# Two layers of a hybrid decoder trunk on one core: the order in which one DMA queue issues weights and modulation tiles

## The chip, the core and the metric

The kernel runs on one core of a Trainium2 chip. A core has TensorE (matrix products, PE in the profile), VectorE (DVE), ScalarE (ACT), GpSimd (POOL), SyncE (SP, which here issues nearly all transfers from HBM) and 16 DMA engines. The metric is the device time of one launch in microseconds (us); lower is better.

## The reference

Two layers work on x, 256 tokens of width 2048, in f32. With c one vector of 2048, each layer computes

```
mod = silu(c) @ ada_w + ada_b            # ada_w: 2048 x 12288, six vectors of 2048: shift, scale, gate, twice
h = rms_norm(x, norm_mix) * (1 + sc_a) + sh_a
p = h @ w_in                             # inputs of three attention mixers
o = concat(rms(mla(p)), rms(fox(p)), rms(nsa(p)))
x = x + gt_a * (o @ w_out)
h = rms_norm(x, norm_mlp) * (1 + sc_m) + sh_m
x = x + gt_m * (square(relu(h @ mlp_w1)) @ mlp_w2)    # mlp width 8192
```

and a last RMSNorm follows. The product `silu(c) @ ada_w` has a single row, but its weights are 100 MB per layer; the other weights are some 215 MB per layer. Every weight is read from HBM once.

## The kernel before, in words

**Pieces.** All products of the tokens with weights are cut into 828 pieces, numbered Q = 0 to 827 in `PIECES`: 158 in the front part of each layer (`ORDER`: input projection, latent projections, compression, output projection) and 256 in each MLP. A piece is two blocks of 128 rows of a weight by at most 512 columns (512 KB where it is full). It passes four stations: SP loads it into `w_raw` (a ring of `RAW` = 5 slots, line 613); ACT rounds it into `w_hi` (line 724); DVE subtracts, `w_lo = w_raw - w_hi` (line 1188); PE multiplies with both (lines 1659 to 1661, or 1679 and 1680 for the compression weights). `w_hi` and `w_lo` are rings of `RING` = 4 slots: ACT starts on piece Q when PE is done with Q - 4. A slot of `w_raw` is free when the DVE instruction of piece Q - 5 is done (`lo_done`).

**Modulation tiles.** The product with `ada_w` is done on DVE: 384 tiles of 128 x 1024 (512 KB), n = 0 to 383, sixteen to a block. Each is multiplied by one column of silu(c) and added to `ada_acc` (line 1125 for the first tile of a block, 1128 for the others); PE then sums `ada_acc` over the partitions (line 1569). The first 64 tiles go through a ring of `FIRST_RING` = 8 slots in `arena` (line 628). All later ones go through `ada_raw`, which has 2 slots (line 633): tile n can be loaded when tile n - 2 is used (`ada_used`). All loads of tiles and pieces are issued by SP, in one queue.

**The order on DVE.** `SIDE` lists for each piece the further steps after it; DVE does `w_lo` of piece Q, then the steps of `SIDE[Q]`. `DVE_ORDER` is that list, reduced to the entries ("lo", Q) and ("ada", n). Tiles 0 to 15 come ahead of piece 0, tiles 16 to 63 lie three to a piece among pieces 1 to 17, and the later blocks are spread over 14 to 70 pieces each: 16 over 16 or 17 pieces at the end of the first layer's front part and at the start of its MLP, eight blocks of 16 over 21 pieces each (with 3 pieces between) in the rest of that MLP. After piece 572 (the second layer's MLP) there are tiles for the first 54 pieces only.

**The order on SP.** `LOADS` (lines 366 to 377) has one entry per load: the place in `DVE_ORDER` of the step that frees its slot, the place of the step that reads it, the kind, the number. SP goes through `LOADS` in order; `load_piece` and `load_ada` wait for the slot's semaphore and issue the transfer. A wait holds up everything behind it on SP. The list is sorted by its first member, the freeing step, so that SP waits for events in the order in which DVE makes them.

Of the kernel before, what the change touches and what calls it, by code (L numbers as in the profile page):

```python
# [366 lines left out]
LOADS = []  # L367
# [3 lines left out]
for n in range(TILES):  # L371
# [2 lines left out]
    else:  # L374
        free = DVE_AT["ada", n - 2] if n >= FIRST_TILES + 2 else DVE_AT["ada", n - FIRST_RING]
    LOADS.append((free, DVE_AT["ada", n], "ada", n))
LOADS.sort()


Y_SLOT, Y_NO, Y_BEFORE = {}, {}, {}  # L380
# [1413 lines left out]
```

How the kernel before makes its waits and increments, by code:

```python
        def free_y(eng, l, name):  # L582
            before = Y_BEFORE[l, name]
            if before is not None and before[0] == l and before[1] in Y_LAST_T:
                eng.wait_ge(*t_is_full(l, Y_LAST_T[before[1]]))
                if before[1] in Y_LAST_SPLIT:
                    eng.wait_ge(split_done, split_value(l, Y_LAST_SPLIT[before[1]]))
# [6 lines left out]
            def load_piece(Q):  # L595
# [6 lines left out]
                        src = mlp_w2[l, s * D + 256 * p:s * D + 256 * p + 256, 512 * (ch - 4):512 * (ch - 4) + 512]  # L602
                    n = 512
                elif chunk == "cw1":
                    w1, n = (cmp_k_w1, cmp_v_w1)[p // 16], 512
                    src = w1[l, 256 * (p % 16):256 * (p % 16) + 256, :]
                else:
                    w, c0, n, a_ = CHUNKS[chunk]
                    row = P * OUT_KT[p] if w == "w_out" else 256 * p
                    src = w_rows[w][l, row:row + 256, c0:c0 + n]
                if Q >= RAW:
                    sp.wait_ge(lo_done, Q - RAW + 1)
                sp.dma_start(w_raw[:, Q % RAW, :, 0:n], src.rearrange("(k p) n -> p k n", p=P)
                             ).then_inc(raw_landed[Q % RAW], 16)
# [1 line left out]
            def load_ada(n):  # L616
# [8 lines left out]
                if n < FIRST_TILES:  # L625
                    if n >= FIRST_RING:
                        sp.wait_ge(ada_used, n - FIRST_RING + 1)
                    sp.dma_start(first_raw[:, n % FIRST_RING, :].rearrange("p (s d) -> p s d", s=2), src
```

## Time and profile before

| what | value |
|---|---|
| time, median of 3 runs (lowest to highest) | 2499.36 us (2497.02 to 2499.56) |
| the profiled execution's own time | 2493.08 us |
| its span, first to last instruction | 2490.8 us |
| TensorE clock granted, mean over the span | 0.984 of full |
| busy: PE, DVE, ACT | 96%, 71%, 48% of the span |
| read from HBM | 629.85 MB |

How to read it: the profile is one execution; "idle before" is the time an engine stood still ahead of an instruction, with what ended it. Busy PE is modelled from pipelined matmuls. "To landing" is the time from a transfer's issue on SP to its semaphore. Transfers of the first 120 us are bound by the DMA engines; behind that the DMA engines have room.

### The profile page before, as it was taken

The numbers are of one execution on the slowest core, as the hardware profiler recorded it, in microseconds if no ns is written. First come the engines' busy times: TensorE is split into PE (matmuls) and PEld (weight loads), VectorE is DVE, ScalarE is ACT, GpSimd is POOL, SyncE is SP. The second block draws the span as 40 slices with busy tenths as digits, with TensorE's granted clock in tenths as the row PEclk, the third lists the DMA queues.
The fourth block names the chain that finished last, engine by engine and source line by source line (L and its number), as shares of the span: only waits on it lengthen the run. The fifth ranks groups of instructions, "written<-read, shape, count | busy, mean of one in ns | idle before, by whom it ended". The sixth has DMA issues, their size and how long they took to land.

```text
span 2490.8 us, 29668 instructions
## 1 busy us (share of the span) xinstructions
PE 2388.0 (96%) x11277; PEld 1977.1 (79%) x11277; DVE 1773.2 (71%) x2116; ACT 1202.6 (48%) x1646; POOL 23.7 (1%) x50
## 2 busy tenths in 40 slices
PE   3799999989999999999999999999999999999998
PEld 3678888767778878888888888877788888888887
DVE  7988988678777777787777788676566545555555
ACT  3256555435534434434445566454563453443453
POOL 1000000000000000000000000000000000000000
PEclk9799999999999999999999999999999999999999
DMA  9979986688889989889877788466577656656664
GB/s 367 380 244 349 311 272 216 224 278 278 296 305 314 309 289 324 295 298 317 297 248 254 260 286 272 144 208 212 187 243 245 193 179 198 190 185 195 183 190 144
DMA packets 318612, 633.91 MB, mean 254 GB/s; under 512 B 20428, under 2 KB 41352, under 8 KB 317832
## 3 DMA queue, kind: packets, MB, share of 16 engines
q1 hardware_dynamic: 314432, 625.49, 75.7%
q10 hardware_dynamic: 4040, 6.54, 0.8%
q8 instruction: 90, 1.47, 0.2%
q14 instruction: 50, 0.41, 0.0%
HBM read 629.85 MB, written 2.10 MB: 254 GB/s over the span
## 4 chain that ended last, share of the span: by engine, by line
PE 78%; DVE 10%; DMA 7%; issue 3%; ACT 2%; SPq 0%; POOL 0%; ACTq 0%; POOLq 0%; DVEq 0%
PE acc L1659 17%; PE acc L1661 17%; PE acc L1660 17%; PE pair L1659 6%; PE pair L1661 6%; PE pair L1660 6%; DMA ada_raw<-in_ada_w 4%; DVE ada_acc L1128 4%; DVE w_lo L1188 3%; DMA arena<-in_ada_w 2%; PE bank_T L1524 1%; PE bank_T L1569 1%; PE pair L1707 1%; PE acc L1679 1%; PE acc L1680 1%
## 5 line engine op out<-in xcount | busy, mean ns | idle before, releaser
L1188 DVE TENSOR_TENSOR w_lo<-w_raw,w_hi 128x1024 fp32r<-128x1024 f32 (+3 forms) x828 | 978.5, 1191 | 321.4 <-ACT w_hi L724 320.6
L724 ACT ACTIVATE w_hi<-w_raw 128x1024 fp32r<-128x1024 f32 (+3 forms) x828 | 849.1, 1032 | 719.4 <-PE acc L1661 460.1
L1659 PE MATMUL acc<-w_hi,hT_hi 128*128 128x512 f32 (+3 forms) x1536 | 611.2, 398 | 28.6 <-DVE hT_lo L1302 15.2
L1661 PE MATMUL acc<-w_lo,hT_hi 128*128 128x512 f32 (+3 forms) x1536 | 591.8, 385 | 0.0
L1660 PE MATMUL acc<-w_hi,hT_lo 128*128 128x512 f32 (+3 forms) x1536 | 590.5, 384 | 0.0
L1128 DVE SCALAR_TENSOR_TENSOR ada_acc<-ada_raw,silu_c,ada_acc 128x1024 f32<-128x1024 f32 x300 | 383.9, 1280 | 99.2 <-DMA ada_raw<-in_ada_w 97.7
L1659 PEld LDWEIGHTS acc<-w_hi,hT_hi 128*128 128x128 f32 x1536 | 293.1, 191 | 90.9 <-DVE hT_lo L1302 18.0
L1661 PEld LDWEIGHTS acc<-w_lo,hT_hi 128*128 128x128 f32 x1536 | 292.2, 190 | 56.5
L1660 PEld LDWEIGHTS acc<-w_hi,hT_lo 128*128 128x128 f32 x1536 | 293.5, 191 | 52.2 <-issue 1.7
L1659 PE MATMUL acc<-w_hi,uT_hi 128*128 128x512 f32 (+1 forms) x720 | 283.3, 394 | 0.9 <-DVE w_lo L1188 0.9
L1661 PE MATMUL acc<-w_lo,uT_hi 128*128 128x512 f32 (+1 forms) x720 | 279.6, 388 | 0.0
L1660 PE MATMUL acc<-w_hi,uT_lo 128*128 128x512 f32 (+1 forms) x720 | 279.5, 388 | 0.0
L1659 PE MATMUL pair<-w_hi,hT_hi 128*128 128x512 f32 (+1 forms) x448 | 178.9, 399 | 15.9 <-DVE w_lo L1188 15.9
L1661 PE MATMUL pair<-w_lo,hT_hi 128*128 128x512 f32 (+1 forms) x448 | 174.1, 389 | 0.0
L1660 PE MATMUL pair<-w_hi,hT_lo 128*128 128x512 f32 (+1 forms) x448 | 173.8, 388 | 0.0
L1659 PEld LDWEIGHTS acc<-w_hi,uT_hi 128*128 128x128 f32 x720 | 135.2, 188 | 30.0 <-DVE w_lo L1188 2.2
L1661 PEld LDWEIGHTS acc<-w_lo,uT_hi 128*128 128x128 f32 x720 | 135.1, 188 | 27.9
L1660 PEld LDWEIGHTS acc<-w_hi,uT_lo 128*128 128x128 f32 x720 | 135.2, 188 | 27.7 <-issue 1.0
L1659 PE MATMUL pair<-w_hi,uT_hi 128*128 128x512 f32 (+1 forms) x352 | 137.0, 389 | 2.4 <-DVE w_lo L1188 2.3
L1661 PE MATMUL pair<-w_lo,uT_hi 128*128 128x512 f32 (+1 forms) x352 | 136.2, 387 | 0.0
L1660 PE MATMUL pair<-w_hi,uT_lo 128*128 128x512 f32 (+1 forms) x352 | 136.1, 387 | 0.0
L1659 PEld LDWEIGHTS pair<-w_hi,hT_hi 128*128 128x128 f32 x448 | 86.0, 192 | 35.0 <-DVE w_lo L1188 19.4
(259 smaller groups left out, 2038.0 us busy)
## 6 DMA issues: line engine op xcount, KB each, us to landing
w_raw<-in_mlp_w SPq DMA_DIRECT2D x512, 512.0 KB, 4.8
ada_raw<-in_ada_w SPq DMA_DIRECT2D x320, 512.0 KB, 5.1
w_raw<-in_w_in SPq DMA_DIRECT2D x112, 512.0 KB, 4.9
arena<-in_ada_w SPq DMA_DIRECT2D x64, 512.0 KB, 11.3
w_raw<-in_w_out SPq DMA_DIRECT2D x64, 512.0 KB, 5.0
w_raw<-in_nsa_cmp_k_w SPq DMA_DIRECT2D x32, 512.0 KB, 5.1
w_raw<-in_nsa_cmp_v_w SPq DMA_DIRECT2D x32, 512.0 KB, 5.1
w_raw<-in_w_in SPq DMA_DIRECT2D x16, 388.0 KB, 4.8
```

What stands on the lines that cost most here:

```text
L724: a.activation(w_hi[:, Q % RING, :, 0:n], w_raw[:, Q % RAW, :, 0:n], ACT.Copy).then_inc(hi_done, 1)
L1128: ins = v.scalar_tensor_tensor(ada_acc[:], raw, silu_c[:, kt:kt + 1], ada_acc[:], ALU.mult, ALU.add)
L1188: v.tensor_tensor(w_lo[:, Q % RING, :, 0:n], w_raw[:, Q % RAW, :, 0:n], w_hi[:, Q % RING, :, 0:n].bitcast(F32), ALU.subtract).then_inc(lo_ ...
L1524: mm = pe.transpose(bank[:, k, P * m:P * m + P], halves[m], ident[:])
L1569: mm = pe.matmul(flat_[:, k:k + 1], ada_acc[:, P * k:P * k + P], ones[:, 0:1], start=True, stop=True)
L1659: pe.matmul(o, st_hi[:, kt + k, tok], wh, start=first and k == 0, stop=False)
L1660: pe.matmul(o, st_lo[:, kt + k, tok], wh, start=False, stop=False)
L1661: mm = pe.matmul(o, st_hi[:, kt + k, tok], wl, start=False, stop=last and k == 1)
L1679: pe.matmul(acc[1][:, j, :], st, w_hi[:, Q % RING, k, :], start=kt == 0, stop=False)
L1680: mm = pe.matmul(acc[1][:, j, :], st, w_lo[:, Q % RING, k, :], start=False, stop=kt == 31)
L1707: mm = pe.matmul(o, NQ[:, h, qt], k_[:, h // 4, 0:keys], start=True, stop=True)
```

## The change

`LOADS` is sorted by its second member, the place in `DVE_ORDER` of the step that reads the load, in place of the step that frees its slot. Slots, waits and semaphores are the same; 861 of the 1212 loads stand at another place of the list.

```
@@ -374,7 +374,7 @@
     else:
         free = DVE_AT["ada", n - 2] if n >= FIRST_TILES + 2 else DVE_AT["ada", n - FIRST_RING]
     LOADS.append((free, DVE_AT["ada", n], "ada", n))
-LOADS.sort()
+LOADS.sort(key=lambda load: load[1])
```

Two stretches of the list, worked out from the code (w is a piece, a a tile):

```
before: a57 a58 a59 w19 a60 a61 a62 w20 a63 a64 a65 w21
after:  a57 w16 a58 a59 a60 w17 a61 a62 a63 w18 w19 w20

before: w148 a141 w149 a142 w150 a143 w151 a144 w152 a145 w153 a146 a147 w154
after:  w148 a144 a145 w149 a146 w150 a147 w151 a148 w152 a149 w153 a150
```

## Rows read from the trace of the kernel before

**Rows 1.** The page: busy time by engine, and PE's share in 40 slices.

```profile
PE 2388.0 (96%) x11277; PEld 1977.1 (79%) x11277; DVE 1773.2 (71%) x2116; ACT 1202.6 (48%) x1646; POOL 23.7 (1%) x50
PE   3799999989999999999999999999999999999998
```

**Rows 2.** Stretches: from:to, length, busy by engine (instructions), clock, DMA share, GB/s.

```profile
30.00:120.00 90.00, 64.69 (x280) 56.00 (x281) 80.40 (x79) 31.90 (x46) 0.35 (x1) 0.83 1.05 384
500.00:580.00 80.00, 68.78 (x299) 54.24 (x298) 58.19 (x63) 35.78 (x59) 1.10 (x2) 0.96 0.76 249
...
660.00:1280.00 620.00, 617.43 (x2824) 509.89 (x2824) 473.91 (x431) 276.29 (x293) 0.00 (x0) 1.00 0.89 302
1900.00:2400.00 500.00, 500.00 (x2247) 413.13 (x2246) 262.71 (x226) 226.94 (x236) 0.00 (x0) 1.00 0.62 188
```

**Rows 3.** Waits of engines, whole span: us in total, times, longest us.

```profile
ACT w_hi L724 <- PE acc L1661: 460.1, 312, 4.9
...
DVE ada_acc L1128 <- DMA ada_raw<-in_ada_w: 97.7, 73, 3.2
```

**Rows 4.** Waits of the SP queue, whole span.

```profile
SPq L613 <- DVE w_lo L1188: 1322.6, 810, 8.4
SPq L633 <- DVE ada_acc L1128: 537.0, 298, 7.3
```

**Rows 5.** Waits between 30 and 130 us.

```profile
DVE ada_acc L1128 <- DMA arena<-in_ada_w: 5.1, 9, 1.2
```

**Rows 6.** DVE in order of time, 121 to 126 us: start, us, instruction, idle before.

```profile
121.71 1.29 DVE L1128 SCALAR_TENSOR_TENSOR ada_acc<-arena,silu_c,ada_acc 128x1024 f32<-128x1024 f32 x1 [0.23 <-DMA arena<-in_ada_w]
122.91 2.36 DVE L1188 TENSOR_TENSOR w_lo<-w_raw,w_hi 128x1024 fp32r<-128x1024 f32 x2
125.18 0.16 DVE L1142 TENSOR_TENSOR ada_A<-bank_T,bcols 128x8 f32<-128x8 f32 x1
```

**Rows 7.** SP, ACT in order of time, 668 to 673 us.

```profile
668.48 0.34 SPq L633 DMA_DIRECT2D ada_raw<-in_ada_w  x1
669.62 0.37 SPq L613 DMA_DIRECT2D w_raw<-in_mlp_w  x1
670.81 0.34 SPq L633 DMA_DIRECT2D ada_raw<-in_ada_w  x1
...
672.18 1.05 ACT L724 ACTIVATE w_hi<-w_raw 128x1024 fp32r<-128x1024 f32 x1
```

**Rows 8.** Time to landing: tiles in the whole span, pieces 570:620, pieces 620:660.

```profile
DMA to landing us min/median/max: 3.4/5.1/11.1
DMA to landing us min/median/max: 3.8/5.2/6.2
DMA to landing us min/median/max: 4.8/5.3/7.2
```

**Rows 9.** DVE in order of time, around seven late pieces (first, two, last).

```profile
222.59 0.74 DVE L1125 TENSOR_SCALAR ada_acc<-ada_raw,silu_c 128x1024 f32<-128x1024 f32 x1
...
526.08 0.75 DVE L1125 TENSOR_SCALAR ada_acc<-ada_raw,silu_c 128x1024 f32<-128x1024 f32 x1 [3.50 <-PE bank_T L1569]
...
530.64 1.28 DVE L1128 SCALAR_TENSOR_TENSOR ada_acc<-ada_raw,silu_c,ada_acc 128x1024 f32<-128x1024 f32 x1 [1.28 <-DMA ada_raw<-in_ada_w]
531.84 1.22 DVE L1188 TENSOR_TENSOR w_lo<-w_raw,w_hi 128x1024 fp32r<-128x1024 f32 x1
...
619.82 1.28 DVE L1128 SCALAR_TENSOR_TENSOR ada_acc<-ada_raw,silu_c,ada_acc 128x1024 f32<-128x1024 f32 x1 [1.07 <-DMA ada_raw<-in_ada_w]
...
901.82 1.28 DVE L1128 SCALAR_TENSOR_TENSOR ada_acc<-ada_raw,silu_c,ada_acc 128x1024 f32<-128x1024 f32 x1
```

**Rows 10.** PE in order of time: first matmuls of pieces 60, 150, 179, 276.

```profile
230.24 0.50 PE L1679 MATMUL acc<-w_hi,uT_hi 128*128 128x512 f32 x1 [0.32 <-DVE w_lo L1188]
...
533.20 0.47 PE L1659 MATMUL acc<-w_hi,hT_hi 128*128 128x512 f32 x1 [0.76 <-DVE w_lo L1188]
...
628.51 0.50 PE L1659 MATMUL acc<-w_hi,hT_hi 128*128 128x512 f32 x1
...
911.26 0.50 PE L1659 MATMUL pair<-w_hi,uT_hi 128*128 128x512 f32 x1 [0.82 <-DVE w_lo L1188]
```

More of the change, by code:

```diff
@@ L376 @@
     LOADS.append((free, DVE_AT["ada", n], "ada", n))
-LOADS.sort()
+LOADS.sort(key=lambda load: load[1])
 Y_SLOT, Y_NO, Y_BEFORE = {}, {}, {}
```

## The prediction, written before the changed kernel ran

> **What bounds the kernel now.** I read the page first, then the time by stretches, the waits (of the engines, then of SP), the landing times, and last single instructions at the places where PE has little in hand.
>
> The page has PE busy for 2388.0 of 2490.8 us; the slices show that the missing 103 us lie mostly in the first two, with an 8 for 498 to 560 us and one at the end [rows 1]. By stretches: from 30 to 120 us PE works 64.7 of 90 us while the DMA engines are full (share 1.05, 384 GB/s) and DVE is busy for 80.4; from 500 to 580 us, the seam between front part and MLP of the first layer, PE works 68.8 of 80; in the rest of that MLP 617.4 of 620, though DMA still runs at 0.89; in the second layer's MLP all of 500, with DMA at 0.62 [rows 2]. So PE is the bound, except at the start (transfers and DVE) and at the seams (DVE in turn with PE).
>
> Two waits say how the pieces are covered. ACT waits 460.1 us for PE before it makes w_hi: the weight is there and the 4-slot ring behind it is full, which is the reserve. DVE waits 97.7 us for modulation tiles, 73 times, nearly all while PE doesn't stop [rows 3]: the two-slot ring of the tiles has little reserve, and the pieces' ring pays for it. SP is idle most of the time, waiting for lo_done (1322.6 us) and ada_used (537.0 us) [rows 4]; each transfer leaves the moment its slot is free. That is what the change gives up.
>
> **The change, part by part.** No instruction is added or removed; 1212 loads, the same slots and semaphores. Three effects.
>
> 1. *The start.* Up to tile 63 the DMA engines are full, so a load lands when the bytes ahead of it have passed. Tile 63 stood behind pieces 0 to 20, now behind 0 to 17: pieces 18, 19 (524 KB each) and 20 (328 KB) are 1.376 MB less, at 384 GB/s [rows 2] 3.6 us. Tile 63 was waited for at 121.71 [rows 6] and now lands at 118.1. But DVE next makes w_lo of pieces 18 and 19, which now stand behind it: 118.1 + 2 x 1.37 (524 KB at 384 GB/s) = 120.8, then w_hi 1.05 [rows 7] and w_lo 1.22, plus 0.1 of semaphores: 123.2, where it was 122.91 + 2.36 = 125.27 [rows 6]. Gain 2.1 us. DVE waited 5.1 us for tiles in this phase [rows 5], so its own work isn't what stops the gain. Bounds: nothing (if another step sets piece 18) to 3.6 us (all of it). I take 2.1, the one that the rows of this spot give step by step. Tiles 31 and 47 gain likewise, but it is the same 1.376 MB, and not added.
>
> 2. *Pieces lose lead.* A tile n of the two-slot ring can't be issued before tile n - 2 is used. In the new list every piece that DVE reads after tile n stands behind it, with its slot free or not. From the order of the list: 355 of 828 pieces are issued later than before, 18 in the first 24, 88 in the rest of the first front part, 204 in the first MLP, 45 in the second front part, none in the second MLP. Their lead falls from 5 pieces to 3 or 4. Behind such a piece wait its w_hi on ACT (and ACT's later steps: evacuations, exponentials), its w_lo on DVE (and the tiles and additions behind that), and then PE. The few loads that ACT issues aren't behind SP.
>
> A held piece is ready for PE at: use of the freeing tile + 0.4 (SP issues the tile first, 0.34 [rows 7]) + landing L + w_hi 1.05 + w_lo 1.22 [rows 9] + 0.1 = +2.8 + L. PE loses what that is past its first matmul on the piece. Worked for piece 150: it stands behind tile 146, which waits for tile 144, used at 526.08 + 0.75 = 526.83; PE starts at 533.20 [rows 9, 10]: 6.4 us, so it is late when L is over 3.6. I did this for all held pieces and took the worst of each cluster (a later one is shifted with it). With L = 6.0 (need 8.8):
>
> piece 60: 223.33 to 230.24, 6.9, late 1.9
> piece 150: 6.4, late 2.4
> piece 155: 543.98 to 551.29, 7.3, late 1.5
> piece 165: 578.94 to 586.46, 7.5, late 1.3
> piece 179: 621.10 to 628.51, 7.4, late 1.4
> piece 211: 716.84 to 724.07, 7.2, late 1.6
> piece 276: 903.10 to 911.26, 8.2, late 0.6
>
> [rows 9, 10] have the first, the second, the fifth and the last of the seven. Sum 10.7 us; the others are covered by PE's reserve.
>
> Why 6.0: pieces land in 5.2 and 5.3 us (medians) in these stretches, the quickest in 3.8, the slowest in 7.2 [rows 8]. Before, a piece left 1.14 us behind a tile (668.48, 669.62 [rows 7]), now 0.37, so 0.8 us more of the tile's bytes are ahead of it: 5.2 + 0.8. Bounds of the sum: with the quickest of 3.8 it is 0.2; with 7.2 each of the seven has 1.2 more and some ten more pieces come over, 26 us.
>
> 3. *Tiles land sooner.* The piece that used to leave 1.2 us ahead of a tile (669.62 before 670.81 [rows 7]) now leaves with the tile before, so a tile finds up to 0.8 us less in front of it. DVE waits for tiles just where PE's reserve is gone (1.28 at 530.64, 1.07 at 619.82 [rows 9]). Bounds: nothing, to 5 us (0.8 at each of the six late places from 150 on). I take 2: most of it is used up by the wait for the piece, which is later.
>
> The skill bears on 2. The rows of SP show waits of 1322.6 and 537.0 us on its own sequencer [rows 4]. The Trainium skill, DMA: Bandwidth & Descriptors, "Anatomy of one DMA — SWDGE (gpsimd) path", says that DMA engines never wait on semaphores: the wait is on the issuing sequencer, ahead of dispatch; by that rule a held tile stops every piece behind it though its slot is free, and the trace agrees. The same section fits a transfer as about 2.0 us + bytes/436e3; for 524 KB that is 3.2 us, an estimate from that page, and with it as L no piece would be late and the sum would be -2.1 - 2 = -4. The quickest tile of the trace took 3.4 and the median 5.1 [rows 8], so in this traffic the measured L decides.
>
> Sum: -2.1 + 10.7 - 2 = +6.6 us. The profiled execution took 2493.08 and would be 2499.7; it lies 6.3 under the median of the runs, 2499.36, on which I put the forecast: 2506.
>
> **The rivals.**
>
> *A. The cover holds (not slower).* One mechanism, at pieces 150 to 211: the tile comes first and lands in time, DVE runs ahead, and the pieces' later issue falls into PE's reserve. For it: PE stops hardly at all in the first MLP [rows 2] and ACT has 460 us of waiting for PE [rows 3]; L under 5.2 is enough to halve the sum (5.3, from the same list). Against it: the reserve is at 0.1 us just at these places (PE ends its idle time on w_lo at 230.24, 533.20, 911.26 [rows 10]). With L about 4.9: start -3.6, pieces +3.5, tiles -5: -5 us, 2494. It decides from L = 5.2 downward.
>
> *B. DVE falls behind for good (much slower).* Three tiles now make a loop: use of tile n - 2, issue 0.4, landing of the piece behind tile n, w_hi 1.05, 0.1, w_lo 1.22, tile n + 1 1.28: 4.1 + L. PE needs 2.67 us a piece (500 us for 2247/12 pieces [rows 2]), 3.5 us a tile at 16 tiles to 21 pieces. With L = 6.0 the loop gives 3.4 us a tile, just enough; with 7.2 it gives 3.75, and loses 4 us in each of nine blocks, of which the reserve takes most, and PE some 1 to 2; with the 26 us above less 2.1 and 2 it is +22 to +30: 2525. Against: the median piece isn't near 7.2.
>
> *C. It does nothing that shows*, since nearly all of the 355 pieces have more than 8.8 us: 2499.4.
>
> **How the numbers follow.** No change can be told within 0.2%, 5 us of the median (2494.4 to 2504.4). My forecast, 0.55, has its own range +1 to +14 (2500 to 2513); some 0.37 of that is over +5, 0.18 within. A 0.27: 0.12 faster by over 5 us, 0.15 within. B 0.14, slower. C 0.04, within. Together: faster 0.12, same 0.37, slower 0.51. The range for 8 in 10 runs from -6 (A) to +20 (the near end of B): 2493 to 2519.
>
> **What would show it.** Right: in the trace after, SP's waits on ada_used grow at the cost of those on lo_done; DVE's wait for tiles falls well under 97.7 us, and ACT's waits for w_raw transfers, and DVE's for w_hi, grow; the ada_A instruction of 125.18 comes at 123; PE first idles on w_lo near pieces 60, 150 to 186 and 211; the second layer's MLP is unchanged to 1 us. Wrong: PE without new idle time from 220 to 920 us (A), or with more in every block up to 1280 (B); landings of pieces that stay at 5.2 or under though they leave with a tile; a start that isn't earlier at tile 63, which would mean that slots, not bytes, pace it.

## The result: 14 us slower, and the profile after

| | before | after |
|---|---|---|
| median (5 runs each) | 2498.19 us | 2509.48 us |
| lowest to highest | 2495.92 to 2499.56 | 2507.36 to 2512.72 |
| ratio, 95% interval | | 1.0056 (1.0044 to 1.0067): 11 to 17 us |
| profiled execution, its span | 2493.08, 2490.8 | 2507.36, 2505.1 |

The median lies in the range (2493 to 2519) and the sign is as forecast; the size is about twice the 6.6 us of the sum, which forecast 2506. (The ratio, taken round by round on one chip, makes 14 us; the two medians alone differ by 11.3.)

The page of the changed kernel, PE's line, PE's slices and the two groups of section 5 whose idle time moved (columns: busy us, mean ns, then idle us before and what ended most of it):

```profile
PE 2388.8 (95%) x11277; PEld 1972.7 (79%) x11277; DVE 1783.9 (71%) x2116; ACT 1201.6 (48%) x1646; POOL 23.8 (1%) x50
PE   3799999989999999999999999999999999999998
...
L724 ACT ACTIVATE w_hi<-w_raw 128x1024 fp32r<-128x1024 f32 (+3 forms) x828 | 851.0, 1033 | 886.4 <-DMA w_raw<-in_mlp_w 336.7
...
L1128 DVE SCALAR_TENSOR_TENSOR ada_acc<-ada_raw,silu_c,ada_acc 128x1024 f32<-128x1024 f32 x300 | 383.6, 1279 | 17.3 <-DMA ada_raw<-in_ada_w 15.6
```

PE works as long as before [rows 1]; only its idle time grew. DVE's waits for tiles fell from 97.7 us [rows 3] to 15.6. In their place ACT waits for pieces (13.8 us for those of the MLPs before, 336.7 now). The engines' waits over the whole span (us in total, times, longest), and those of the SP queue:

```profile
DVE w_lo L1188 <- ACT w_hi L724: 428.8, 438, 4.2
ACT w_hi L724 <- DMA w_raw<-in_mlp_w: 336.7, 181, 8.4
ACT w_hi L724 <- PE acc L1661: 273.7, 197, 3.6
```

```profile
SPq L613 <- DVE w_lo L1188: 996.0, 518, 8.8
SPq L633 <- DVE ada_acc L1128: 732.5, 248, 14.3
```

ACT's wait for PE, the sign of a full reserve, fell from 460.1 us [rows 3] to 273.7; SP's waits moved from lo_done to ada_used [rows 4].

The stretches that answer to [rows 2], shifted with the program (500 to 584 answers to 500 to 580, 669 to 1294 to 660 to 1280, 1914 to 2414 to 1900 to 2400; their ends fit to 1 to 3 us, so the exact loss is read from the table below):

```profile
30.00:120.00 90.00, 65.19 (x290) 56.66 (x291) 82.99 (x82) 30.20 (x45) 0.60 (x1) 0.85 1.05 384
500.00:584.00 84.00, 69.10 (x286) 53.45 (x285) 56.02 (x60) 34.89 (x57) 1.10 (x2) 0.92 0.68 231
...
669.00:1294.00 625.00, 618.02 (x2818) 507.70 (x2817) 478.76 (x429) 270.51 (x289) 0.00 (x0) 1.00 0.86 299
1914.00:2414.00 500.00, 500.00 (x2247) 413.16 (x2246) 262.89 (x227) 226.88 (x235) 0.00 (x0) 1.00 0.62 189
```

This stretch of the second MLP is the same to a matmul (2247); most of the time went at the seam and in the first MLP. To place it, I took the start of PE's first matmul on each piece in both traces; the difference, after less before, is PE's delay. Its steps, beside the terms of the sum:

| pieces | delay before and after the stretch | step | predicted |
|---|---|---|---|
| 0 to 18 | 0 to -1.9 | -1.9 | -2.1 |
| 26 | -1.9 to -0.4 | +1.5 | 0 |
| 60 to 66 | -0.6 to +1.6 | +2.2 | +1.9 |
| 126 to 127 | +1.2 to +4.3 | +3.0 | 0 |
| 127 to 131 | +4.3 to -1.4 | -5.6 | 0 |
| 144 to 146 | -1.4 to +0.7 | +2.1 | 0 |
| 150 | +0.7 to +3.2 | +2.5 | +2.4 |
| 151 to 161 | +3.2 to +5.5 | +2.3 | +1.5 |
| 162 to 186 | +5.5 to +6.0 | +0.5 | +2.7 |
| 187 to 234 | +6.0 to +10.4 | +4.4 | +1.6 |
| 235 to 413 | +10.4 to +13.9 | +3.5 | +0.6 |
| 414 to 420 | +13.9 to +12.3 | -1.6 | 0 |
| 570 to 576 | +12.7 to +14.3 | +1.6 | 0 |

(Smaller steps between the rows of the table make up -0.2 us.) In five of its rows the granted clock differs between the two profiles. For 127 to 131, the stretch before, and the same one after:

```profile
440.00:460.00 20.00, 17.70 (x68) 13.10 (x68) 9.31 (x22) 6.97 (x16) 0.00 (x0) 0.74 0.43 148
```

```profile
441.00:461.00 20.00, 19.02 (x98) 14.86 (x97) 13.96 (x28) 10.87 (x23) 0.00 (x0) 1.00 0.48 161
```

The column behind POOL is the granted clock: 0.74, against 1.00. In the old order PE had stood still for 2.3 us (until 447.16) and then ran at 1.2 GHz for 10 us. In the new one it stood still for 1.0 us at the same matmul and had 2.4 GHz all the time. So of the -5.6 us, 1.3 is the shorter stop and 4.7 the clock (0.4 of loss is in between). The +3.0 ahead of it is no matter of the clock: PE stands still for 2.8 us there (see "What the sum left out"). The clock has the steps at 414 to 420 (0.93 before, 1.00 after) and at 570 to 576 (1.00, 0.95), 1.6 of the 2.3 us at 151 to 161 (between 560 and 580 us it is 1.00 before, 0.91 after) and 1.2 of the 2.1 us at 144 to 146 (between 500 and 520 us it is 0.91 before, 0.83 after). So one pair of profiles holds steps of 1.2 to 4.7 us of either sign that are the clock's. They add up to about -2: at the same clock the two spans would lie some 16 us apart instead of 14.3, against 6.6 in the sum.

Over the runs the clock isn't what costs: its mean is 0.985 in the five runs of the changed kernel, and 0.984 to 0.985 on each of three chips in the 55 runs of the kernel before that the experiments have beside them.

### The profile page after: what moved, and what is told of

It is laid out like the page before. It is cut to its first block, busy times and chain, and to the rows that moved or that the text cites. A ratio compares the mean times of both kernels' runs of the same rounds, so it can differ in the third digit from the quotient of the medians.

```text
span 2505.1 us, 29668 instructions
## 1 busy us (share of the span) xinstructions
PE 2388.8 (95%) x11277; PEld 1972.7 (79%) x11277; DVE 1783.9 (71%) x2116; ACT 1201.6 (48%) x1646; POOL 23.8 (1%) x50
## 4 chain that ended last, share of the span: by engine, by line
PE 71%; DVE 10%; DMA 10%; ACT 4%; issue 4%; SPq 1%; POOL 0%; ACTq 0%; DVEq 0%; POOLq 0%
PE acc L1659 16%; PE acc L1661 16%; PE acc L1660 16%; DMA w_raw<-in_mlp_w 5%; PE pair L1659 5%; PE pair L1661 5%; PE pair L1660 5%; DVE ada_acc L1128 4%; DVE w_lo L1188 3%; DMA w_raw<-in_w_in 2%; ACT w_hi L724 2%; PE bank_T L1524 1%; PE bank_T L1569 1%; DMA w_raw<-in_w_out 1%; PE pair L1707 1%
## 5 line engine op out<-in xcount | busy, mean ns | idle before, releaser
L724 ACT ACTIVATE w_hi<-w_raw 128x1024 fp32r<-128x1024 f32 (+3 forms) x828 | 851.0, 1033 | 886.4 <-DMA w_raw<-in_mlp_w 336.7
L1128 DVE SCALAR_TENSOR_TENSOR ada_acc<-ada_raw,silu_c,ada_acc 128x1024 f32<-128x1024 f32 x300 | 383.6, 1279 | 17.3 <-DMA ada_raw<-in_ada_w 15.6
L1660 PEld LDWEIGHTS acc<-w_hi,uT_lo 128*128 128x128 f32 x720 | 135.3, 188 | 27.6 <-issue 1.0
```

The costliest lines, as they stand in the source:

```text
L724: a.activation(w_hi[:, Q % RING, :, 0:n], w_raw[:, Q % RAW, :, 0:n], ACT.Copy).then_inc(hi_done, 1)
L1128: ins = v.scalar_tensor_tensor(ada_acc[:], raw, silu_c[:, kt:kt + 1], ada_acc[:], ALU.mult, ALU.add)
L1660: pe.matmul(o, st_lo[:, kt + k, tok], wh, start=False, stop=False)
```

## The experiments

All ratios are to the kernel before on the same chip. The code is shortened: it shows the lines that matter.

**The change in parts.** A mixed order: the loads that a condition picks keep their set of places in the old list, but fill these in the order of reading.

```
 LOADS.sort()
+NEED = [i for i, load in enumerate(LOADS) if <condition>]
+for i, load in zip(NEED, sorted([LOADS[i] for i in NEED], key=lambda load: load[1])):
+    LOADS[i] = load
```

*The start alone*: condition `load[3] < 64 if load[2] == "ada" else load[3] < 24`.

> The new order for tiles 0 to 63 and pieces 0 to 23 alone, the old one behind them. Theory 1 (pieces lose lead behind held tiles; the start gains because tile 63 has 1.376 MB less ahead of it): the gain of the start stands alone, 2 us faster than before, all of it in hand by piece 12 or 18. Theory 2 (the loss is contention: transfers that leave together land later): the same, since the start's queue is full in either order. If the start's gain came from the order behind it, no change.

Measured: 2494.61 against 2497.98, ratio 0.9986 (0.9973 to 0.9998), 3.5 us faster, with an interval of 0.5 to 6.7. The delay at piece 18 is -1.7 in its profile, as in the change (-1.9). So the gain of the start stands alone. Its size is not settled by the runs: they were also granted a little more clock (mean 0.9854 against 0.9842, and 0.0012 of the span is 3.0 us).

*All but the start*: the condition negated.

> The old order for tiles 0 to 63 and pieces 0 to 23, the new one behind them. If the two parts simply add: 16 us slower than before (14 of the change plus the 2 of the start), with the steps of PE's delay at the same pieces as in the change (24 to 30, 60 to 66, 144 to 162, 211 to 231, 348, 396 to 403).

Measured: 2513.52, ratio 1.0060 (1.0042 to 1.0078), 15 us slower. With the start's -0.14% that makes +0.46%, where the change has +0.56%: the two parts add within their intervals.

*The seam alone* (pieces 132 to 164, tiles 128 to 159) and *the first MLP alone* (pieces 187 to 413, tiles 176 to 335):

> The new order for pieces 132 to 164 and tiles 128 to 159 alone, the seam of the first layer; the old order everywhere else. PE's delay in the profiles grew by 5.5 us from piece 144 to 160 in the change. If the steps of the delay are local causes: 4 to 7 us slower than before. My prediction's landing of 6.0 gave 3.9 here. If the loss at the seam needs the held pieces ahead of it, under 2.

> The new order for pieces 187 to 413 and tiles 176 to 335 alone, the first layer's MLP behind its first chunks; the old order everywhere else. In the profiles PE's delay grew by 7.8 us there in the change (pieces 211 to 234, 348, 396 to 403). If these are local: 6 to 10 us slower than before. By my prediction's landing of 6.0 it would be 2.2; by the measured 6.8 about 5. If the first MLP only loses because it comes in late from the seam, under 2.

Measured: the seam 2508.44 against 2496.26, ratio 1.0041 (1.0026 to 1.0056), 10 us; the MLP 2504.98, ratio 1.0031 (1.0018 to 1.0045), 8 us.

The 10 us aren't the seam's price. The mixed list of that run has two places that neither list has: `a126 a128 a127` (tile 127 stands behind tile 128, whose slot waits for tile 126) and `w165 w166 w164`. Its profile shows both. SP takes 7.7 us from the first to the last of three tile issues in a row, DVE waits 3.9 us for tile 127, and PE stops behind that (lines of this run's kernel stand 11 further down):

```profile
432.61 7.67 SPq L644 DMA_DIRECT2D ada_raw<-in_ada_w  x3
```

```profile
451.56 0.80 PE L1708 MATMUL pair<-arena 128*128 128x128 f32 x2 [6.32 <-ACT arena L885]
```

There the delay grows by 4.0 us, and by 2.8 at piece 164. The run's clock is lower too (0.9832 against 0.9848, worth some 4 us at most). What can be compared is the stretch from piece 143 to 161: the delay grows by 6.9 us in this profile, and by the same 6.9 in the change. So the seam's loss is local, and some 7 us in either profile, with the clock's part in it. That -0.14%, +0.41% and +0.31% make +0.58% is therefore partly chance; pieces 24 to 131 and the second front part were in none of the three.

The MLP's loss is local as well. In the profile of that run the delay grows from 5.6 at piece 186 to 12.9 at 413, by 7.3 us (7.8 in the change; 12.1 in the run with all but the start, whose list is the same there). The 5.6 ahead of it lie where the order is the old one, 3.3 of them at pieces 150 to 162, where the clock is 0.91 in place of 1.00: that part differs from run to run.

**The lead alone.** `RING, RAW = 4, 5` becomes `4, 3`, old order.

> The order before (by freeing step), but w_raw has 3 slots in place of 5: each piece leaves as soon as its slot is free, yet no earlier than three pieces ahead; nothing is held behind a tile and nothing leaves in a burst. Theory 1 (the lead alone counts): as slow as the change or slower, 12 to 30 us over before, with the loss at the seam and in the first MLP; the second MLP without a loss of more than 2 us, since its pieces land in 4.2 to 4.8 us. Theory 2 (bursts): within 5 us of before.

Measured: 2560.0, ratio 1.0241 (1.0217 to 1.0265), 60 us slower, twice the upper end. The direction is theory 1's, and so is the second MLP: PE's delay is 70.1 us both at piece 570 and at the end. But most of the loss is not where the change has its own: 33.5 us up to piece 162 and 27.6 in the second front part, where a narrow or compression piece occupies PE for less than 2 us and three pieces of lead are soon gone. In the stretch that can be compared, pieces 192 to 413, three slots cost 6.7 us (delay 35.8 to 42.5), the change 7.8. (Between 187 and 192 three slots cost another 3.3, about half of it where only that run had the lower clock.) A lead of three pieces with landings of 5.3 us is there worth about as much as a held piece with 6.8:

```profile
DMA to landing us min/median/max: 3.6/5.3/7.0
```

```profile
DMA to landing us min/median/max: 4.5/6.8/9.5
```

These are the landings of pieces between 660 and 1280 us, first with three slots, then in the changed kernel; before, the median of the same stretch was 5.7.

**The tiles' slots.** One slot goes from w_raw to ada_raw (4 and 3), in either order; the buffers, semaphores and slot numbers follow.

```
-RING, RAW = 4, 5
+RING, RAW = 4, 4
-        free = DVE_AT["ada", n - 2] if n >= FIRST_TILES + 2 else ...
+        free = DVE_AT["ada", n - 3] if n >= FIRST_TILES + 3 else ...
```

> The new order, with one slot moved from w_raw (4 in place of 5) to ada_raw (3 in place of 2). A tile now waits for tile n - 3, so pieces are held behind it about one piece less. Theory 1: most of the loss goes, 0 to 5 us over before. Theory 2 (bursts of tile and pieces): the bursts stay, 10 to 14 us over before.

> The old order (by freeing step) with 4 slots of w_raw and 3 of ada_raw: the partner of the run with the same slots in the new order, 2483.9. Theory 1: holding matters little once tiles wait for n - 3, so the two orders differ by the start's 2 us and little else: 0 to 4 us slower than that partner, 10 to 14 faster than before. Theory 2 (bursts cost even there): faster than the partner by 3 us or more.

Measured: new order 2483.89, ratio 0.9944 (0.9926 to 0.9963), 14 us faster than before; old order 2486.89, ratio 0.9961 (0.9945 to 0.9976), 10 us faster. The first came out better than even theory 1 had it (0 to 5 us over before): I had counted only the loss that would vanish, not the 97.7 us of tile waits. With a third slot the order costs nothing (3 us in favour of the new one, about the start's part; the intervals overlap). The same list that costs 14 us with two slots is harmless with three: what costs is a queue waiting for a slot that comes free too late. With three slots and the new order, the first MLP has PE busy throughout:

```profile
660.00:1280.00 620.00, 620.00 (x2844) 514.53 (x2843) 481.68 (x436) 275.53 (x293) 0.00 (x0) 1.00 0.88 304
```

**The size of the landing.** From tile 66 on only half of each tile is loaded, so part of the modulation is left out; in either order.

```
-sp.dma_start(ada_raw[:, n % 2, :]..., src)
+part = 2 if n < FIRST_TILES + 2 else 1
+sp.dma_start(ada_raw[:, n % 2, :]...[:, 0:part, :], src[:, 0:part, :])
```

> The order before, but from tile 66 on only the first half of each tile (256 KB) is loaded; DVE works on the whole slot as before, so the values of the modulation are left out in part. Partner of the next run. Tiles and pieces land sooner; DVE's 98 us of waits for tiles fall to under 40; PE gains where its reserve was at nothing: 3 to 8 us faster than before.

> The changed kernel with the same halved tiles (part of the modulation's values left out). Waits and order are those of the change, only the bytes of the held-up burst are less: landing of pieces some 1 us shorter (under 6 where it is 6.8). Theory 1 with landing as its size: by my sum a landing of 5.5 instead of 6.8 us takes two thirds of the loss away: 2 to 7 us slower than the run with half tiles in the old order. If the loss were the wait alone, whatever the landing: 12 to 16 us slower than that run.

Measured: old order 2474.47, ratio 0.9915 (0.9892 to 0.9938), 21 us faster than before, where 3 to 8 were expected. In its profile 9.2 us are gained by piece 131, 4.9 more by 163 and 4.8 more by 413, so the tile transfers cost more than I had thought, and not at one place. New order 2484.75, ratio 0.9948 (0.9934 to 0.9962), 10 us slower than its partner (8 by the ratios): it misses both expectations, 2 to 7 and 12 to 16, and lies between them. The profiles tell why it is between. Between 660 and 1280 us ACT still waits for pieces, 125 times, but PE no longer stops (from the new order with half tiles: a wait, and the stretch):

```profile
ACT w_hi L725 <- DMA w_raw<-in_mlp_w: 211.1, 125, 6.1
```

```profile
500.00:580.00 80.00, 66.89 (x283) 52.01 (x282) 57.39 (x62) 36.99 (x59) 1.10 (x2) 0.94 0.56 182
660.00:1280.00 620.00, 620.00 (x2846) 514.73 (x2845) 479.46 (x436) 276.03 (x292) 0.00 (x0) 1.00 0.72 244
```

PE's delay between the partners is 12.5 us at piece 156 and 12.6 at the end. So the first MLP's loss is one of size: with landings of pieces of 5.6 us (4.6 with half tiles in the old order) the reserve covers the hold, with 6.8 it doesn't. The seam's loss is there at either landing (the delay grows by 8.5 us between pieces 143 and 156, part of it at a lower clock): PE has no reserve at these places [rows 10], and a held piece shifts it.

**One ring.** The 7 slots of both kinds as one ring, filled in the order of reading; the first 64 tiles keep theirs.

```
+LOADS.append((-1, place of the reading step, what, n)); LOADS.sort(key=lambda load: load[1])
+RAW_NO[what, n] = len(shared)                       # slot: RAW_NO % 7
+RAW_BEFORE[what, n] = shared[-7]                    # whose use frees it
+sp.wait_ge(lo_done if before[0] == "w" else ada_used, before[1] + 1)
```

> The 5 slots of w_raw and the 2 of ada_raw as one ring of 7, filled and freed in the order in which DVE reads; the first 64 tiles keep their own ring of 8. Freeing order and reading order are then one order, and every load has a lead of seven loads: 7 pieces where there are no tiles, 3 to 4 pieces and as many tiles where they alternate. Theory 1 (lead and landing): DVE no longer waits for tiles and hardly for w_hi, the seam and the first MLP gain, and the compression stretch loses nothing since its lead grows: 10 to 20 us faster than before. Theory 2 (bursts): no burst is left, the same 10 to 20 us. If neither lead nor bursts matter (the difference is the granted clock alone): within 5 us of before.

Measured: 2472.13 against 2497.47, ratio 0.9905 (0.9886 to 0.9923), 24 us faster than before (19 to 28), a little over the 10 to 20 expected, and the fastest of all that do the whole work. In one ring the order of freeing is the order of reading, so no transfer can be held behind a slot that comes later than its own. DVE waits for no tile of these blocks; the seam gains 7.3 us (pieces 143 to 156 in its profile), and the first MLP has no idle PE:

```profile
500.00:580.00 80.00, 72.35 (x331) 57.88 (x330) 66.07 (x72) 41.49 (x65) 1.10 (x2) 1.00 0.82 280
...
660.00:1280.00 620.00, 620.00 (x2841) 514.70 (x2840) 476.41 (x431) 273.80 (x290) 0.00 (x0) 1.00 0.89 305
```

That is 331 matmuls between 500 and 580 us where the kernel before had 299 [rows 2].

**The clock in these times.** The mean granted clock of the runs differs too. What it can be worth has a bound: 1 less the clock, times the span, which is 2.5 us for each 0.001. (Between the runs of the kernel before, 0.001 goes with 1.2 us, so the true part is likely less.) One ring: 0.9885 against 0.9847, at most 10 of the 24 us. Three tile slots: 0.9870 and 0.9869 against 0.9842 and 0.9847, at most 7 of 14 and 6 of 10. Half tiles in the old order: 0.9878 against 0.9847, at most 8 of 21. The runs of the first MLP alone have no difference (0.9847, 0.9848), nor has the change. So part of what these kernels gain may be the clock that PE keeps when it stops less often; no run separates the two.

## Why the prediction was right, and where its size was off

**The start: right.** Tile 63 was to land at 118.1 and landed at 118.3; the w_lo of pieces 18 and 19 were to end at 123.2. DVE in order of time, changed kernel:

```profile
117.82 2.67 DVE L1128 SCALAR_TENSOR_TENSOR ada_acc<-arena,silu_c,ada_acc 128x1024 f32<-128x1024 f32 x2
120.78 2.59 DVE L1188 TENSOR_TENSOR w_lo<-w_raw,w_hi 128x1024 fp32r<-128x1024 f32 x2 [0.29 <-ACT w_hi L724]
123.28 0.16 DVE L1142 TENSOR_TENSOR ada_A<-bank_T,bcols 128x8 f32<-128x8 f32 x1
```

The ada_A step of 125.18 [rows 6] comes at 123.28, 1.9 us sooner. The run with the start alone agrees, with its wide interval.

**The held pieces: the mechanism right.** Piece 150 is the worked example. SP, ACT and PE in order of time:

```profile
527.55 0.37 SPq L633 DMA_DIRECT2D ada_raw<-in_ada_w  x1
527.96 0.47 SPq L613 DMA_DIRECT2D w_raw<-in_w_out  x1
```

```profile
533.93 1.06 ACT L724 ACTIVATE w_hi<-w_raw 128x1024 fp32r<-128x1024 f32 x1 [8.65 <-DMA w_raw<-in_w_out]
```

```profile
536.39 0.47 PE L1659 MATMUL acc<-w_hi,hT_hi 128*128 128x512 f32 x1 [3.27 <-DVE w_lo L1188]
```

It leaves 0.4 us behind the tile that held it, lands 6.0 us later (527.96 to 533.93), and PE begins 2.5 us later than [rows 10] has it, counted from the delay at piece 149; 2.4 was predicted. Of this the Trainium skill's rule on waits (DMA: Bandwidth & Descriptors, "Anatomy of one DMA — SWDGE (gpsimd) path": the issuing sequencer waits, never the DMA engine) is borne out: piece 150's slot was free 17.9 us before it left (w_lo of piece 145 ended at 510.07). That section's fit, made for the gpsimd path, gives 3.2 us for such a transfer (an estimate from that page), by which there would have been no loss. It is not what a transfer takes in this traffic: piece 150 took 6.0.

**The step that was off: the landing of 6.0 us, in the first MLP.** I took 5.2 from the stretch 570 to 620 us and added 0.8. At the seam that holds. Behind 660 us the kernel before already had 5.7, and the burst made it 6.8 (9.5 at most). For pieces 187 to 413 my list gives 2.2 us with a landing of 6.0, about 5 with 6.8, and 7.9 was measured: so the choice of L explains about half of what is missing there, and the rest is open. The row nearest in time to the first late pieces isn't the row of the pieces 100 us on. The burst itself is part of it. Around piece 219, SP:

```profile
746.01 1.90 SPq L613 DMA_DIRECT2D w_raw<-in_mlp_w  x1
747.96 0.47 SPq L633 DMA_DIRECT2D ada_raw<-in_ada_w  x1
748.47 1.02 SPq L613 DMA_DIRECT2D w_raw<-in_mlp_w  x2
```

```profile
754.12 1.06 ACT L724 ACTIVATE w_hi<-w_raw 128x1024 fp32r<-128x1024 f32 x1 [8.40 <-DMA w_raw<-in_mlp_w]
755.21 1.23 DVE L1188 TENSOR_TENSOR w_lo<-w_raw,w_hi 128x1024 fp32r<-128x1024 f32 x1 [4.18 <-ACT w_hi L724]
```

The issue at 746.01 alone took 1.90 us on SP (0.37 in [rows 7]), and piece 219 landed 8.1 us after it. ACT stood still for 8.4 us and DVE for 4.2, more than PE's reserve.

**What the sum left out: the work behind a held piece on ACT.** At three places PE stands still not for a weight but for an evacuation (ACT copies a result of PE out of a bank, `bank_T` here, that PE then needs free). The evacuation stands on ACT behind the w_hi of a held piece, here 27, 128 and 145. The first is at piece 26, the second at piece 127, the third at pieces 143 and 144. ACT and PE at each:

```profile
148.92 1.06 ACT L724 ACTIVATE w_hi<-w_raw 128x1024 fp32r<-128x1024 f32 x1 [3.20 <-DMA w_raw<-in_w_in]
...
433.61 1.06 ACT L724 ACTIVATE w_hi<-w_raw 128x1024 fp32r<-128x1024 f32 x1 [5.28 <-DMA w_raw<-in_w_out]
...
507.75 1.06 ACT L724 ACTIVATE w_hi<-w_raw 128x1024 fp32r<-128x1024 f32 x1 [2.76 <-DMA w_raw<-in_w_out]
```

```profile
150.76 0.66 PE L1524 MATMUL bank_T<-ident,ybuf 128*128 128x128 f32 x4 [1.29 <-ACT ybuf L746]
...
436.12 0.66 PE L1524 MATMUL bank_T<-ident,arena 128*128 128x128 f32 x4 [2.80 <-ACT arena L771]
...
509.59 0.66 PE L1524 MATMUL bank_T<-ident,arena 128*128 128x128 f32 x4 [2.61 <-ACT arena L746]
```

Before, PE waited at none of the three. Together these are 6.7 us of stops, of which 3.2 are given back by shorter waits just behind (1.3 at 447.16, 1.9 at 511.46 of the old order). The run with all but the start has them at the same three matmuls (0.65, 2.89 and 3.60 us). I had named what is queued behind a held piece on ACT and then priced only PE's wait for weights: that term of the sum stood at nothing.

**What the sum had too much of.** The two places at 165 and 179 were to cost 2.7 and cost 0.5: tiles land in 4.0 us there (5.0 before) and DVE, which was late by waiting for them, makes up for it. This is the relief that I had put at 2 us over all. It isn't sure even there: with the same list at these pieces, the run with all but the start loses 3.4 us between 162 and 186. Elsewhere the 82 us of tile waits that vanished came back as waits for w_hi (DVE's wait for ACT grew by 108 us). In the change's profile the 2.2 us too much here hide part of what was left out above, so that the forecast came as near as it did is in part luck.

**The rivals.** A (the cover holds) is what 162 to 186 does in the change's profile, and what half tiles do for the whole MLP; it isn't the sum. B (the three-tile loop) needed L of 7.2 and would have shown in every block: with 6.8 it shows at the end of some (219 to 231, 348, 396 to 404), so its mechanism may take part there; no run tests it apart. C is excluded by the interval.

**What stays open.** How much of the seam's loss is the hold and how much the clock behind PE's new stops: of the 6.9 us between pieces 143 and 161, some 2.8 lie where the changed kernel had more of the lower clock (0.83 against 0.91, 0.91 against 1.00, see above), but I have one profile of each. About half of the first MLP's shortfall against the sum (5.7 us) is open, and it differs between profiles of the same list (7.3 to 12.1 us). The 3 us between the two orders with three tile slots aren't settled either.

## What to carry to other kernels

When the rings behind one in-order queue are short, sort it by the events that it waits for. If all its loads share one ring, both orders are the same, and a slot goes to whoever reads next; here the same 7 slots, as one ring, gave 24 us. In this kernel the reading order paid only at the start, where the queue is bound by bytes and not by slots, and did no harm once the small ring had three slots. A partial change of such a list can make an order that neither whole has; look at its borders before its time is read. When a held transfer is priced, take the landing from the stretch where it happens, with the burst that the hold itself makes, and price every in-order engine that the held load stands in front of, not only the last one.

## What the runs showed of the hardware

- 512 KB transfers that leave 0.4 us behind one another land later than the same ones spaced by 1.1 us, at the same load (302 and 299 GB/s): median 6.8 against 5.7 us; with half the tile bytes 5.6 against 4.6. Between 660 and 1290 us 22 of 359 issues on SP take over 0.6 us, the longest 1.9; before, 1 of 362.
- After PE has stood still for about 2 us the granted clock may fall for the next 3 to 10 us, or not, in the same stretch of the same work. PE's stop of 1.91 us ahead of piece 416 (1316.87 before, 1330.72 after) is followed by the lower clock before and not after; the stop of 2.25 us at 1762.80 before and 1775.53 after, by the lower clock only after. Each cost 1.6 us. The stop of 2.3 us at 447.16, with 10 us of the lower clock, cost 4.7. One pair of profiles can't tell such steps from an edit's without the clock's column.
- In the 55 runs of the kernel before, compared chip by chip, a run whose mean clock is lower by 0.001 takes 1.2 us longer on average (the runs lie between 2491 and 2506 us, the clocks between 0.981 and 0.989).
